# A fused 512-token block of a recurrent, state-space and mixture network: where its modulation rows are computed and how its experts gather their tokens

## What is computed

```python
def adaln_mod(cond, w, b):
    m = jnp.einsum('...d,de->...e', jax.nn.silu(cond), w) + b
    return jnp.split(m[..., None, :], 6, axis=-1)
...
sh1, sc1, g1, sh2, sc2, g2 = adaln_mod(c, ada_w[l], ada_b[l])
csh1, csc1, cg1, csh2, csc2, cg2 = adaln_mod(c_ctx, ada_w[l], ada_b[l])
hl = rms_norm(x, norm1_pre[l]) * (1 + sc1) + sh1
hc = rms_norm(ctx, norm1_pre[l]) * (1 + csc1) + csh1
mc, ml = mixer(hc, hl, p, rows, ctx_out)
x = x + g1 * rms_norm(ml, norm1_post[l])
h2 = rms_norm(x, norm2_pre[l]) * (1 + sc2) + sh2
x = x + g2 * rms_norm(ec_moe(h2, router[l], exp_w1[l], exp_w3[l], exp_w2[l]), norm2_post[l])
...
def ec_moe(h, router, w1, w3, w2):
    cap = EC_CAPACITY * n // N_EXPERTS
    gate, idx = lax.top_k(jnp.swapaxes(aff, 1, 2), cap)
    xe = h[bidx, idx]
    hid = jax.nn.silu(jnp.einsum('becd,edf->becf', xe, w1)) * jnp.einsum('becd,edf->becf', xe, w3)
    ye = jnp.einsum('becf,efd->becd', hid, w2) * gate[..., None].astype(h.dtype)
    return jnp.zeros_like(h).at[bidx, idx].add(ye)
```

## Time and profile before

| | |
|---|---|
| median of 3 runs | 5348.11 us (5346.15 to 5348.35) |
| profiled execution, its own time | 5346.22 us |
| its span | 5344.4 us |
| TensorE busy | 4823.2 us (90%) |
| VectorE, ScalarE, GpSimd busy | 2126.1, 1298.8, 426.6 us |
| mean granted TensorE clock | 0.942 |
| read from memory | 468.47 MB, 92 GB/s over the span |

### The profile page before, as it was taken

The page is one execution under the profiler, slowest core; times in us unless marked ns, Lnnn a source line. Parts: engine busy times, 40 slices in busy tenths (PEclk is TensorE's granted clock), DMA queues, the critical chain, the costliest instruction groups (busy, mean ns, idle before and its releaser), DMA issues.

```text
span 5344.4 us, 80218 instructions
## 1 busy us (share of the span) xinstructions
PE 4823.2 (90%) x33872; PEld 2939.7 (55%) x33872; DVE 2126.1 (40%) x3904; ACT 1298.8 (24%) x2400; POOL 426.6 (8%) x386
## 2 busy tenths in 40 slices
PE   8899999988988969979888898999999998989999
PEld 2466666666555544454332554544677554544777
DVE  2455555553354460031111335463343235473333
ACT  0233333342222210010000123232232123232222
POOL 0011111110231230000000000010000000020000
PEclk9899899998999989989999899999999999989999
DMA  6000000000101004226998211013221211113321
GB/s 250 27 18 18 16 18 18 4 7 30 55 32 40 24 29 168 83 80 254 419 419 354 96 68 61 35 45 124 110 80 48 95 61 60 40 40 124 110 95 48
DMA packets 70701, 494.63 MB, mean 93 GB/s; under 512 B 8771, under 2 KB 9027, under 8 KB 29251
## 3 DMA queue, kind: packets, MB, share of 16 engines
q1 hardware_dynamic: 70342, 489.49, 23.7%
HBM read 468.47 MB, written 21.00 MB: 92 GB/s over the span
## 4 chain that ended last, share of the span: by engine, by line
PE 76%; DVE 8%; issue 7%; DMA 5%; ACT 2%; POOL 1%; PEldq 0%; PEld 0%; SPq 0%; POOLq 0%; DVEq 0%; ACTq 0%
PE ps L224 73%; DMA upper<-in_ew 4%; PE ps L227 3%; DVE upper L235 2%; ACT upper L282 1%; DVE upper L259 1%; DVE upper L243 1%; DVE lower L235 1%; POOL upper L3259 1%; DVE lower L243 1%; DVE upper L251 1%; DMA lower<-in_ada 0%; ACT lower L282 0%; DVE upper L239 0%; DVE lower L251 0%
## 5 line engine op out<-in xcount | busy, mean ns | idle before, releaser
L224 PE MATMUL ps<-lower 128*128 128x512 f32 (+10 forms) x6512 | 1977.7, 467 | 94.5 <-issue 25.1
L224 PEld LDWEIGHTS ps<-lower 128*128 128x128 f32 (+3 forms) x6512 | 998.6, 198 | 793.0 <-issue 605.8
L224 PE MATMUL ps<-upper 64*64 64x64 f32 (+8 forms) x14224 | 895.9, 260 | 144.9 <-DVE upper L251 48.5
L282 ACT ACTIVATE upper<-ps 128x512 f32<-128x512 f32 (+6 forms) x963 | 445.5, 484 | 2063.6 <-PE ps L224 1388.1
L224 PEld LDWEIGHTS ps<-upper 64*64 64x64 f32 (+4 forms) x14224 | 649.1, 149 | 480.1 <-issue 263.9
L224 PE MATMUL ps<-lower,upper 64*64 64x64 f32 (+6 forms) x7216 | 816.8, 325 | 68.0 <-DMA lower<-in_ew 25.6
L224 PE MATMUL ps<-rounded 128*128 128x512 f32 x3072 | 724.8, 398 | 30.7 <-DVE rounded L235 23.1
L224 PEld LDWEIGHTS ps<-rounded 128*128 128x128 f32 x3072 | 586.9, 191 | 167.7 <-ACT rounded L282 26.3
L224 PEld LDWEIGHTS ps<-lower,upper 64*64 64x64 f32 (+3 forms) x7216 | 415.4, 145 | 413.3 <-issue 369.1
L224 PE MATMUL ps<-upper,lower 128*128 128x512 f32 (+4 forms) x1200 | 510.6, 575 | 16.2 <-DVE lower L243 5.6
L282 ACT ACTIVATE upper<-upper 128x768 f32<-128x768 f32 (+10 forms) x615 | 323.1, 531 | 668.8 <-DVE upper L255 167.5
(11 more groups left out here) (78 smaller groups left out, 2113.6 us busy)
## 6 DMA issues: line engine op xcount, KB each, us to landing
lower<-in_ew SPq DMA_DIRECT2D x144, 1024.0 KB, 12.3
upper<-in_ew SPq DMA_DIRECT2D x48, 1024.0 KB, 13.7
lower<-in_b0f SPq DMA_DIRECT2D x16, 2048.0 KB, 8.1
lower<-in_b1f SPq DMA_DIRECT2D x16, 2048.0 KB, 7.7
lower<-in_ada SPq DMA_DIRECT2D x12, 2048.0 KB, 9.6
lower<-in_wrkv SPq DMA_DIRECT2D x8, 1728.0 KB, 7.9
lower<-in_b0g SPq DMA_DIRECT2D x8, 1536.0 KB, 6.7
gad<-upper SPq DMA_DIRECT2D x48, 256.0 KB, 2.0
```

The costliest lines, as they stand in the source:

```text
L224: return self.e.matmul(out, lhsT, rhs, start=start, stop=stop)
L282: self.e.activation(out, in_, func, bias=bias, scale=scale, accum_out=accum).then_inc(line.up(*event), 1)
```

## The change

1. A modulation block is worked by quarters: of the 512 columns each quarter q of 128 is multiplied apart, with its output on partitions 32q and 32q+1, so that the four matmuls of a step use four different 32-column strips of the array (`modulation_tensor`). The bias is added quarter by quarter (four VectorE operations of 2 x 128 for one of 2 x 512). The blocks are loaded as halves of 1 MiB.
2. Only blocks 0 to 3 stay in the start. Blocks 4 to 11 are a new generator, `modulator()`, in RWKV's list, from round 5 to round 44; the row is stored in four pieces, and the second projection set (j = 1) goes on past its shifts only after the store. Their areas lie in the buffers of j = 1, which are free until then; VectorE, ScalarE and GpSimd wait for the store.
3. In the start: of the constants only the identity is loaded ahead, the rest after the blocks; x comes after block 0; the norms no longer wait for `modT`; ScalarE scales three of six token tiles and writes `hC`; `modT` takes four transposes of 128 x 128 in place of sixteen of 2 rows; `wrx`, `wrkv` 0 and block 4 are issued without waiting for the meeting.
4. Experts: `gather(g)` takes the 128 places of one group; group 0's stands ahead, that of g+1 after the second half (f = 1) of g. `P` is made in two pieces (128 places, then 896). `XE` and `YE` are three buffers in rotation.

```diff
+def modulation_tensor(k, pe, ps, i, h):
+
+    w, loaded = k.slot["ada", i, h]
+    w = v3(w, 512)
+    pe.wait_ge(loaded, "ada", i, h)
+    for kk in range(4):
+        for q in range(4):
+            o = pe.mm(ps[32 * q:32 * q + 2, 0:128], k.st.cs3[:, 4 * h + kk, :], w[:, kk, 128 * q:128 * q + 128],
+                      h == 0 and kk == 0, h == 1 and kk == 3)
+    o.then_inc(k.mods.pe.up("mod", i, h), 1)
...
 def start_tensor(k, pe):
...
+    for i in range(3):
+        modulation(i)
+    for c in range(2):
+        turn(c)
+    modulation(3)
...
+    for i in range(4):
+        o = pe.tr(ch(ps, i), ch(k.rw.mod, i))
...
+    for c in range(2, 8):
+        turn(c)
...
 def rwkv_order():
...
+                    if j == 1:
+                        yield from until("stored", 0)
...
+    def modulator():
+        for _ in range(4):
+            yield None
+        for i in range(4, 12):
+            for h in range(2):
+                yield ("ada", i, h)
+                yield None
+            yield ("ada_row", i)
+        yield ("store", 0)
+        for _ in range(3):
+            yield None
+        yield once(("stored", 0))
...
 def rwkv_sync(k, sp):
...
+    def modulation(i):
+        for h in range(2):
+            sp.wait_ge(A.pe, "mod", i - 1, h)
+            src, line = T["ada"][i][:, 2048 * h:2048 * h + 2048], k.line(f"late{h}")
+            sp.e.dma_start(b.adaw[h], src).then_inc(line.up16("ada", i, h), 16)
...
 def moe_tensor(k, pe):
...
+    def gather(g):
+
+        use = ("gather", g)
+        ps = banks.take(use, 2)
+        pe.wait_ge(M.dve, "P", min(g, 1))
+        for kk in range(8):
             for i in range(4):
-                last = pe.mm(ps, k.h2[:, i, 128 * kk:128 * kk + 128], b.P[:, i, 512 * hf:512 * hf + 512], i == 0, i == 3)
...
+                last = pe.mm(ch(ps, kk), k.h2[:, i, 128 * kk:128 * kk + 128], b.P[:, i, 128 * g:128 * g + 128], i == 0, i == 3)
...
-            if g == 0:
-                gather(1, range(4 * f, 4 * f + 4))
-            elif f == 0:
+            if g and f == 0:
                 combine(g - 1)
+        if g < 7:
+            gather(g + 1)
```

More of the change, by code:

```diff
@@ new lines, in start_sync, with load @@
+    areas = [k.wreg[:, 4096 * i:4096 * i + 4096] for i in range(3)]
+    def load(i):
+        for h in range(2):
+            dst = areas[i][:, 2048 * h:2048 * h + 2048] if i < 3 else halves[h]
+            line = k.line(f"ada{i}_{h}")
+            sp.e.dma_start(dst, T["ada"][i][:, 2048 * h:2048 * h + 2048]).then_inc(line.up16("ada", i, h), 16)
+            k.slot["ada", i, h] = (dst, line)
+    load(0)
+    fetch(sp, b.xt[:, 0:4, :], T["x"].rearrange("(i p) d -> p i d", p=128), "x")
+    fetch(sp, b.xt[:, 4:6, :], T["ctx"].rearrange("(i p) d -> p i d", p=128), "ctx")
@@ L614, in rwkv_map @@
     b.outs = outs
+    n = k.mem(late)
+    b.late, b.adaw, b.mod, b.adab = late, [n(2048) for _ in range(2)], n(1536), n(1536)
+    b.cs3 = v3(n(16), 2)
+    assert n.top <= m.top
     b.sg, b.G, b.a, b.P = (m(768) for _ in range(4))
@@ L763, in rwkv_sync @@
             ring.load(("wrkv", j + 2), T["wrkv"][j + 2], P.pe, "lora", j + 2, 1, 1)
+        elif name == "ada_row" and j < 11:
+            modulation(j + 1)
+        elif name == "store":
+            sp.wait_ge(A.dve, "mod", 11)
+            rows = k.mrow.rearrange("o (i q c) -> o i q c", q=4, c=128)
+            for q in range(4):
+                sp.e.dma_start(rows[:, :, q, :], v3(b.mod[32 * q:32 * q + 1, :], 128)).then_inc(k.line("mrow").up16("mrow", q), 16)
         elif name == "tail" and at == [6]:
@@ L1003, in rwkv_tensor @@
             out(*z)
-        else:
+        elif name == "ada":
+            i, h = z
+            if h == 0:
+                at["mod"] = step_banks[0].take(("mod", i))
+            modulation_tensor(k, pe, at["mod"], i, h)
+            if h:
+                step_banks[0].give(("mod", i), k.mods.dve, "mod", i)
+        elif name not in ("ada_row", "store", "stored"):
             prep(name, *z)
@@ L1196, in rwkv_vector @@
             out(*z)
-        else:
+        elif name == "ada_row":
+            modulation_vector(k, v, *z)
+        elif name == "stored":
+            v.wait_ge(k.line("mrow"), "mrow", 3)
+        elif name not in ("ada", "store"):
             prep(name, *z)
@@ L1352, in rwkv_scalar @@
                 a.act(tail.act, b.st, b.st, AF.Exp, "rstd", j, scale=-0.5)
-        else:
+        elif name == "stored":
+            a.wait_ge(k.line("mrow"), "mrow", 3)
+        elif name not in ("ada", "ada_row", "store"):
             prep(name, *z)
@@ L2214, in combine @@
                 v.copy(M.dve, b.acc[:, i, :], ps, "combine", g, i)
-    gather(0, range(8))
+    gather(0)
     for g in range(8):
```

212 lines of the change are left out of this document (107 added, 105 removed).

## The result

Four runs of the changed kernel: median 5264.27 us (5250.39 to 5266.86), beside 5347.13 (5339.17 to 5348.35) for the kernel before. The ratio is 0.9843, 95% interval 0.9823 to 0.9863, so the change makes it 1.6% faster. The forecast was 5261, from 5240 to 5292.

The account below looks back on a forecast made before the run. TensorE, busy 90% of the span, was taken as the bound except in the start, RWKV's first pair and the experts (bound by weights); 5346.2 - 66 + 22 - 41 = 5261 us, range 5240 to 5292.

Parts of the forecast that it names:

- The start, -66: Start of the kernel: RWKV's first product begins at about 49.5 in place of 115.46 us; bounds 60 and 71.
- rival D: Start ends on memory or the norms, not TensorE: 55 for 49.5, time 5267; no chance of its own given.
- Position j = 0, +22: Blocks 4 to 11 of the modulation, worked inside RWKV, cost 22 us, from +8 to +70.
- 17.6 - 5 + 5 + 5: Late halves in RWKV: 17.6 us of TensorE, -5 in waits, +5 VectorE additions, +5 waiting for loads.
- `tri` of j = 0 at 183: Sign in RWKV that the steps are right: `tri` of position 0 at 226.9 - 44 = 183 us.
- The experts, -41: Experts: shorter first gather, first pair 24 us earlier, a gather added to groups 0 to 6; 41 us saved.
- rival B: Experts: the gather is bound by its stationary loads, 0.151 us a pass; time 5279, chance 12%.
- groups 1 to 6 60.7 each: Experts: each of these groups takes 60.7 us, with TensorE at 60.6 and memory at 60.0.
- signs that were to show the steps right: First product at 48 to 52, first expert pair 24 us earlier, groups 60.5 to 61, no `in_ew` wait over 1 us.
- signs of being wrong: Quarter passes over 50 ns, `in_ada` waits above 2 us, clock under 0.7, gathers over 9 us, groups above 62.
- A: Modulation: quarters don't overlap on the array, about +33 us in RWKV and +10 in the start; 5304, chance 7%.
- C: RWKV: late halves starve TensorE, +128 us, time 5389, deciding from about 18.5 us a half; chance 2%.

Follow-up runs that it names:

- no_late: The changed kernel without blocks 4 to 11 of the modulation row (no loads, passes or bias additions for them); 5256.70 us.
- moe_only: The kernel before with only the experts' functions of the change, start and RWKV as before; 5313.96 us.
- late_gather: The changed kernel with the next group's gather moved into the experts' second layer, between its two output halves; 5249.76 us in one execution.
- serial: The changed kernel with two loops swapped, so that the passes of one quarter follow each other; 5269.03 us.

## Why the prediction was right, point by point

**The start, -66: -63.0**, the first product at 52.46 for 49.5. The step was right (TensorE and then the norms, not `wrx`), and of rival D's 5.5 us 3.0 came: the scaling of the norms, which I had done by 33, was done at 36.9, and the turns started at 37.00. Most of this is block 2, which I had multiplied by 28.5; its second half landed at 29.42 and was multiplied at 31.3. The low clock that this wait leaves I had as 1.5 us: in other executions of the same kernel the first product came at 52.7 and 54.2.

**Position j = 0, +22: +5.6** to the output of j = 0. This is the term that was mis-sized. The time of a half was right (1.1 us in the text, 0.98 at the upper clock, 1.82 at the lower), and that the strips work side by side too. The step that failed is the sum, 17.6 - 5 + 5 + 5 (22.6, taken as 22). It lays sixteen halves on a clock that stays as it is; with them it rises from 0.83 to 0.92, and TensorE's busy time grows by 10.2 us where the sum has 17.6. The waits filled are 3.4 us net, for 5, and together the passes cost 6.7 in the stage. The earlier trace rows had the sign of it, 0.74, and so had the r projection's 9.57 us for 16 passes, 0.6 us each; I read the first as the cost of waits, not as a price that falls when the waits are filled. VectorE's additions and the loads, +5 each, were too much as well. The waits for `in_ada` are 1.83 us in all. The additions are on the path at one place that the trace shows: the four at 95.39 stand inside the shift, and with the half behind them the first lora starts 5.6 us after the k projection's end (92.9 to 98.50) where `no_late` has 3.7. From the first product to the output of j = 0, `no_late` takes 276.0 us, the changed kernel 285.7, 283.2 and 286.1, the kernel before 280.1 and with its experts changed (`moe_only`) 276.3: the halves' price is 7 to 10 us there, and 16 in `late_gather`'s low-clock execution. The +5.6 hangs on one pair of executions; these numbers allow +3 to +10.

A milestone was wrong as well. "`tri` of j = 0 at 183" took 226.94 for the first triangular product, but that row begins with eight passes of 64 x 512 in a mixed group, which the changed kernel has behind it. The triangular products of before began at about 235.93 - 3.65 = 232.3, those of the changed kernel at 167.65. The reorder gains nothing by the output of j = 0 (276.0 in `no_late`, 276.3 in `moe_only`).

The pass on a strip took 31 ns, and the prediction's 27 was near. The Trainium skill (TensorE: Matmul & The Clock Gate, Back-to-back issue gap) has a floor of about 25 ns and some 62 ns with one way of decoding; 31 ns lies above the floor and does not agree with the 62, by which a half would be 2 us; the 15 ns of the earlier trace rows lie under both.

**The experts, -41: -34.5.** The first pair 24 us earlier was right to the tenth (10.10 us of gathering for 10.1, comparisons of P at 0.29 us for 0.3), the gather pass as well (7.14 us for 64 from start to next start, 7.4 taken), so rival B is out. The step that failed is "groups 1 to 6 60.7 each": they take 61.84, 1.1 more, 6.8 in six groups. I had TensorE's 60.6 and memory's 60.0 side by side and took the larger, with a hand account of four blocks of lead; the waits for `in_ew` of over 1 us that I had excluded are there (1.33 in the rows above, 1.7 the longest). Its sum was also off: 2398 + 62.5 + 6 x 60.7 + 53 to 55 + 7.1 is 2885 to 2887 and not 2888, so that its own terms make -42 to -44. `late_gather` shows that the same work in another order takes 60.37.

**The sum.** The price of j = 0 was 16 us too high, the gains of the start and of the experts 3 and 6.5 too high, and 4.6 us came from scatter: -16 + 3 + 6.5 - 4.6 is the -11 by which this profiled execution (5250.4) lies under 5261. The median lies 3 over it. That the median was hit so closely is in part luck, errors of opposite sign. Each term lay inside its bounds but that of j = 0, whose +5.6 is 2.4 under its lower bound. Of the signs that were to show the steps right, three missed by a little: the first product at 52.46 for 48 to 52, groups of 61.84 for 60.5 to 61, and the waits for `in_ew`; none of the signs of being wrong came.

**The rivals.** A has its measure in the passes that `serial` and the changed kernel show one by one, B in the gather's passes. C (late halves starve TensorE) had to have halves 18.5 us late; the longest wait for one is 1.63 us.

## What to carry to other kernels

Where a stretch shows a granted clock well under 1 and TensorE waits between short pieces, work put between them can be cheaper than its passes: here 6.7 us for 15.7, part of it from filled waits and more from the clock. Check by leaving it out and by doubling it, and run each more than once. A stage on the edge of two bounds may reach neither (61.84 us a group for 60.6 and 60.0): spread what uses no weights evenly over what does, or the queue's lead is spent at one place and idle at the other. And compare the order of the rows at a milestone before taking it as one.

## What the runs showed of the hardware

- Passes of 128 columns on one strip of 32 columns of the array start 109 ns apart. On four strips in turn a half block of 32 passes takes 0.98 us, 31 ns each, and with one strip's passes after another's, in `serial`, 2.29 us, since two strips then still overlap.
  The Trainium skill (TensorEngine Tiling (Array Packing), Theoretical Speedup) gives up to four times for a side of 32; 32 x 0.109 = 3.5 us against 0.98 is 3.6 times.
- The stage of j = 0 at a mean granted clock of 0.83, 0.92, 0.96 and 0.97 with 0, 15.7, 29.8 and 36.6 us of added passes, one execution each; the length grew by 6.7, 16.0 and 19.2 us, and TensorE's idle time fell from 19.6 to 16.2, 13.8 and 11.7. I had not expected more than half of the first set to be paid for.
- A 5.7 us wait of TensorE at 31 us is followed by low clock: 12 turns take 2.79 us for 1.53, and in some executions, not in others, the 30 turns behind them take 6.40 us for 3.69 and the first product comes 1.7 us later; how the executions differ was not found.
- 64 passes with two columns take 10.6 us together and 0.88 us in eights, 7.0 for 64.
